# Routing inside the last projection chunk of a hybrid decoder step: one table value per row, expert outputs stored by choice and token

## The reference, cut to what matters

```python
hx = rmsnorm(x, norm_ffn)
g_logits = hx @ w_group + b_group            # 4 groups
grp = argmax(g_logits)
in_grp = (hx @ w_router + b_router)[grp]     # 8 experts of that group
top_v, top_i = top_k(in_grp, 2)
gate = softmax(top_v) * softmax(g_logits)[grp]
# each token goes to 2 of 32 experts; rows of one expert are put together
y_e = (silu(x_e @ w_gate[e]) * (x_e @ w_up[e])) @ w_down[e]
x = rmsnorm(x + gate_0 * y(choice 0) + gate_1 * y(choice 1))
```

## Time and profile before

| what | us |
|---|---|
| median of 3 runs | 1857.71 (1856.18 to 1859.96) |
| the profiled execution | 1851.79 |
| its span in the trace | 1850.0 |
| TensorE busy | 1684.7 (91%) |
| VectorE busy | 876.2 (47%) |
| ScalarE busy | 713.0 (39%) |
| GpSimd busy | 369.2 (20%) |
| HBM read and written | 223.16 MB, 65.51 MB |

### The profile page before, as it was taken

One profiled execution on the slowest core, in us unless ns is written; L12 is line 12 of the kernel. 1 busy time (PEld: TensorE's weight loads), 2 busy tenths in 40 slices (PEclk: granted clock), 3 DMA queues, 4 the chain that ended last, 5 costly groups with the idle time before them and its releaser, 6 DMA issues.

```text
span 1850.0 us, 31840 instructions
## 1 busy us (share of the span) xinstructions
PE 1684.7 (91%) x12271; PEld 1561.5 (84%) x12272; DVE 876.2 (47%) x1663; ACT 713.0 (39%) x1234; POOL 369.2 (20%) x323
## 2 busy tenths in 40 slices
PE   5999999999999999999999979999997299999970
PEld 4998998999989999888887869999997299999960
DVE  5533223123122110555666632345324779999857
ACT  5323223222232222344444432313014178888852
POOL 3001002001002135000000000000012147777744
PEclk7999999999999999999999989999999599999995
DMA  6033303304215325232222232224215199999977
GB/s 189 24 95 101 118 24 117 123 13 160 69 40 184 114 84 170 71 112 68 68 64 76 84 114 93 93 76 157 84 73 230 37 336 380 380 376 378 370 275 271
DMA packets 141568, 272.44 MB, mean 147 GB/s; under 512 B 36068, under 2 KB 106988, under 8 KB 129132
## 3 DMA queue, kind: packets, MB, share of 16 engines
q1 hardware_dynamic: 102688, 202.05, 31.8%
q0 software_dynamic: 19280, 48.93, 7.5%
q10 hardware_dynamic: 19488, 19.87, 3.3%
HBM read 223.16 MB, written 65.51 MB: 156 GB/s over the span
## 4 chain that ended last, share of the span: by engine, by line
PE 80%; DVE 6%; DMA 6%; issue 4%; ACT 2%; DVEq 1%; POOL 1%; SPq 0%; ACTq 0%; POOLq 0%
PE pb L761 19%; PE pb L762 18%; PE pb L763 17%; DMA stage<-in_w_gate_e 4%; PE pw L761 2%; PE pw L763 2%; PE pw L762 2%; PE pq L1099 2%; PE pw L1075 2%; DVE wlo L1703 2%; PE pq L835 2%; PE pw L852 1%; PE pq L761 1%; PE pq L763 1%; PE pq L762 1%
## 5 line engine op out<-in xcount | busy, mean ns | idle before, releaser
L761 PE MATMUL pb<-aTh,wlo 128*128 128x352 f32 x1152 | 384.6, 334 | 17.9 <-DVE aTl L2102 8.1
L761 PE MATMUL pb<-whi,aTl 128*128 128x256 f32 (+1 forms) x1296 | 374.4, 289 | 4.8 <-PE pb L763 2.8
L763 PE MATMUL pb<-aTh,whi 128*128 128x352 f32 x1152 | 371.2, 322 | 0.0
L762 PE MATMUL pb<-aTl,whi 128*128 128x352 f32 x1152 | 370.8, 322 | 0.0
L762 PE MATMUL pb<-wlo,aTh 128*128 128x256 f32 (+1 forms) x1296 | 365.4, 282 | 0.0
L763 PE MATMUL pb<-whi,aTh 128*128 128x256 f32 (+1 forms) x1296 | 363.1, 280 | 0.0
L761 PEld LDWEIGHTS pb<-aTh,wlo 128*128 128x128 f32 x1152 | 217.2, 189 | 48.1 <-issue 34.2
L761 PEld LDWEIGHTS pb<-whi,aTl 128*128 128x128 f32 (+1 forms) x1296 | 232.2, 179 | 17.9 <-issue 8.3
L1703 DVE TENSOR_TENSOR wlo<-stage,whi 128x2048 fp32r<-128x2048 f32 x74 | 169.2, 2287 | 142.0 <-ACT whi L1290 142.0
L763 PEld LDWEIGHTS pb<-whi,aTh 128*128 128x128 f32 (+1 forms) x1296 | 233.4, 180 | 1.0
L762 PEld LDWEIGHTS pb<-wlo,aTh 128*128 128x128 f32 (+1 forms) x1296 | 231.9, 179 | 2.0
(11 more groups left out here) (417 smaller groups left out, 2823.1 us busy)
## 6 DMA issues: line engine op xcount, KB each, us to landing
stg<-in_w_down_e SPq DMA_DIRECT2D x32, 1024.0 KB, 12.3
stage<-in_w_in SPq DMA_DIRECT2D x30, 1024.0 KB, 5.4
stage<-in_w_gate_e SPq DMA_DIRECT2D x16, 1024.0 KB, 12.5
stage<-in_w_up_e SPq DMA_DIRECT2D x16, 1024.0 KB, 12.8
stg<-in_w_gate_e SPq DMA_DIRECT2D x16, 1024.0 KB, 13.0
stg<-in_w_up_e SPq DMA_DIRECT2D x16, 1024.0 KB, 13.7
zg_scratch<-go ACTq DMA_DIRECT2D x48, 176.0 KB, 1.9
sgt<-zg_scratch SPq DMA_DIRECT2D x16, 528.0 KB, 3.5
```

What stands on the lines that cost most here:

```text
L761: pe.matmul(out, ll, rh, start=first, stop=False)
L762: pe.matmul(out, lh, rl, start=False, stop=False)
L763: return pe.matmul(out, lh, rh, start=False, stop=last)
```

## The change

The routing becomes part of the last chunk's loop. Each tile's best group and best two experts (`top_two`) are found three iterations after its projection, its ranks (`rank`) four after. TensorE adds two small products for the ranks (`ranks`) into a spare strip of `ZB` and two that place the rows (`placed`), summed over all tiles. The normalised rows are written in their own iteration instead of one later, the transposes come one iteration earlier, and the router has 36 columns. The table has one value for each row, token + 1 + T * choice, from which both columns of `idx` are made (`tables`): outputs are stored at `choice * T + token`, and `slot` is gone. Group weights, overflow counts and two of the weight splits are put elsewhere in the lists of ScalarE and VectorE. GpSimd clears its buffers before it waits for the table, and its expert loop is written out, with columns of `idx` used in place. In the tail SP reloads the outputs as plain blocks. Only the overflow blocks (experts with over 128 rows) keep the copied lists.

The other edits, as a diff (SP, ScalarE, VectorE's first expert, GpSimd):

```diff
-            sp.wait_ge(init_v, 2)
...
+            sp.wait_ge(m_end, 1)
+            for t in range(NT):
+                if t >= NY:
+                    sp.wait_ge(f_a, t - NY + 1)
+                for k, y in enumerate((y1, y2)):
+                    r = k * T + t * 128
+                    sp.dma_start(y[t % NY][0:rows(t), :], ys_d[r:r + rows(t), :]).then_inc(f_y[t % NY], 16)
...
+                if t == 2:
+                    split_hi(N_MOE, 0, 0, lds(N_MOE))
+                if t == NT - 1:
+                    split_hi(N_MOE + 1, 1, 1, lds(N_MOE + 1))
...
-            for m in range(2):
-                split_hi(N_MOE + m, m, m, lds(N_MOE + m))
-            act.wait_ge(r_v, 1)
-            act.activation(ge[:, :, :], ge[:, :, :], ACT.Exp)
-            act.activation(r1[:, 3, :], r1[:, 2, :], ACT.Exp).then_inc(r_a, 1)
...
-            act.wait_ge(r_v, R_END)
+            act.wait_ge(r_v, R_WGT)
+            act.activation(ge[:, :, :], ge[:, :, :], ACT.Exp)
+            act.activation(r1[:, 3, :], r1[:, 2, :], ACT.Exp).then_inc(r_a, 1)
...
+            x_low(0, 0)
+            weights_of_rows()
             slot_lo(PG(1), 1, 0)
-            slot_lo(PD(0), 0, 2)
-            slot_lo(PU(1), 1, 1)
-            x_low(0, 0)
             gated_half(0)
             x_low(1, 1)
+            slot_lo(PD(0), 0, 2)
             hidden(0)
...
+                if isinstance(e, int):
+                    rows_ = column(0, e)
+                else:
+                    rows_ = ixs[par][:, 0:1]
+                    gp.tensor_copy(ixs[par][:, :], column(0, e)).then_inc(e_ix, 1)
+                    gp.wait_ge(e_ix, e - (NE - 1))
+                    gp.sem_inc(carry[2], 1)
                 gp.indirect_dma_start(out=xg[par][:, :], out_offset=None, in_=h2_d,
-                                      in_offset=bass.IndirectOffsetOnAxis(ap=ixs[par][:, 0:1], axis=0),
+                                      in_offset=bass.IndirectOffsetOnAxis(ap=rows_, axis=0),
...
-            gp.wait_ge(r_v, R_END)
             gp.wait_ge(st_x, 16 * NT)
-            for i in range(2):
-                gp.wait_ge(st_h[i], 16 * ((NT + 1 - i) // 2))
             for x in xg:
                 gp.memset(x[:, :], 0.0)
             gp.drain()
+            for i in range(2):
+                gp.wait_ge(st_h[i], 16 * ((NT + 1 - i) // 2))
+            gp.wait_ge(r_v, R_IDX)
             gather(0, 0)
             gather(1, 1)
             gather(2, 0)
             gather(3, 1)
-            with gp.Fori(0, NE // 2 - 2) as i:
-                gather(2 * i + 4, 0)
-                store_y(2 * i, 0)
-                gather(2 * i + 5, 1)
-                store_y(2 * i + 1, 1)
+            for e in range(NE - 4):
+                gather(e + 4, e % 2)
+                store_y(e, e % 2)
...
-            for t in range(NT):
-                n = rows(t)
-                if t >= NY:
-                    gp.wait_ge(f_a, t - NY + 1)
-                for k, y in enumerate((y1, y2)):
-                    gp.indirect_dma_start(out=y[t % NY][0:n, :], out_offset=None, in_=ys_d,
-                                          in_offset=bass.IndirectOffsetOnAxis(ap=slot[0:n, k, t:t + 1], axis=0),
-                                          bounds_check=2 * T - 1).then_inc(f_y[t % NY], 16)
```

More of the change, by code:

```diff
@@ L40 @@
 NI = 3
-TOP, SC_END = 229344, 214048
+TOP, SC_END, KEEP = 229344, 214048, 139296
 NGRP, EPG, NE, FF = 4, 8, 32, 256
@@ L1265, in _ @@
             with pe.If(any_ > 0):
+                pe.wait_ge(e_yc, E(NE - 1))
+                for a in range(2 * NT):
+                    pe.wait_ge(r_o, NT + a + 1)
+                    pe.matmul(pq[:, 0, 0:NOVER], ORo[a % 2][:, :], OBo[a % 2][:, :], start=(a == 0),
+                              stop=(a == 2 * NT - 1)).then_inc(r_r, 1)
                 with pe.Fori(0, NOVER) as j:
@@ L2146, in _, with bc @@
             ve.memset(onesf[:, :], 1.0)
-            def logits(t):
+            ve.memset(Ac[:, 0, :], 0.0)
+            ve.tensor_scalar(thr[:, :], io[:, 0:8], 128.0, 128.0, ALU.mult, ALU.add)
+            ve.memset(big[:, :], float(2 ** 17))
+            ve.tensor_copy(vt[:, 0, :], C("tokid"))
+            ve.scalar_tensor_tensor(out=vt[:, 1, :], in0=C("valid"), scalar=float(T), in1=C("tokid"),
+                                    op0=ALU.mult, op1=ALU.add)
+            ve.drain()
+            def bc(a, shape, *at):
+                for k in at:
+                    a = a.unsqueeze(k)
+                return a.to_broadcast(shape)
@@ L2224, in _ @@
-            ve.drain()
-            for k in range(2):
-                ve.tensor_tensor(O[:, k, :, :], O[:, k, :, :], bc(C("valid"), [128, NT, NE], 2), ALU.mult)
-            ve.memset(Ac[:, 0, :], 0.0)
-            ve.drain()
-            ve.tensor_tensor(A[:, :, :], O[:, 0, :, :], O[:, 1, :, :], ALU.add)
-            ve.tensor_tensor(Ae[:, :, :], O[:, 0, :, :].rearrange("p t e -> p e t"),
-                             O[:, 1, :, :].rearrange("p t e -> p e t"), ALU.add)
-            ve.drain()
@@ L2323, in _ @@
             ve.tensor_copy(ovt[:, :, :], ovf[:, 0:2, :])
-            for m in range(2):
-                split_lo(N_MOE + m, m, m)
-            ve.wait_ge(r_p, 2)
-            found = pw[:, 0, 0:2 * NBLK].rearrange("p (k b) -> p k b", k=2)
-            ve.tensor_scalar(emp[:, :, :], found, 0.0, big[:, 0:1], ALU.is_equal, ALU.mult)
-            ve.drain()
-            ve.scalar_tensor_tensor(out=idx[:, :, :], in0=found, scalar=-1.0, in1=emp[:, :, :],
-                                    op0=ALU.add, op1=ALU.add)
```

341 lines of the change are left out of this document (152 added, 189 removed).

## The result

The changed kernel takes 1848.37 us (median of five runs, 1847.37 to 1850.22) against 1857.82 of the kernel before: a ratio of 0.9948 (0.9933 to 0.9962). It is 9.5 us faster where 24.3 were forecast; 1848.4 lies above the range of 1826 to 1846. The profiled execution took 1847.37 us with a span of 1845.5.

The account below looks back on a forecast made before the run. The prediction took the serial routing before the first gather as delaying the whole expert stage: 12.9 + 6.7 - 2.0 + 1.0 + 5.7 = 24.3 us off the profiled 1851.8, so 1827.5, or 1833.4 as median; range 1826 to 1846.

Parts of the forecast that it names:

- Part 1: Routing inside the last chunk: 6.6 us a tile, chunk 9.6 us longer, table ready 12.9 us earlier, at 1449.2.
- E: Rival: TensorE and VectorE take turns in the chunk, 12 us an iteration, 32 us lost, 1866; chance 0.03.
- Rival B: In the chunk, GpSimd's power lands after the top-two chain: 8.5 us a tile, 11.4 lost, 1845; chance 0.18.
- Part 2: From the table to the first gathered rows: 6.2 us, a gain of 6.7 us.
- 0.1 + 3.0 + 3.1 us: Table to first gathered rows: time before the indirect DMA, the DMA on GpSimd, then its landing; 6.2 us together.
- the exclusion rule: A VectorE instruction with two SBUF inputs and a GpSimd instruction reading SBUF exclude each other, the later one waiting.
- the upper bound of 11.8 us: Longest time from table to first gathered rows, should the 5.5 us gap ahead of GpSimd's copy come back.
- Part 3: First experts: subtractions moved between VectorE's steps make the weight stream late; 2 us charged, bounds 0 and 4.2.
- Part 4: Tail: 1.0 us gained by a last store without copy, 2.9 before the first combine, 2.8 from first to last.

Follow-up runs that it names:

- early_read: The new kernel with VectorE reading the logits out of PSUM at the start of the iteration, ahead of the projection add: 1838.72 us.
- combined: The new kernel with logits read at iteration start, no clearing of gather buffers, new order after the ninth group, second weight split before the last rank: 1833.88 us.
- warm: combined plus 43 products on TensorE that nobody reads, 10 in the chunk's waits and 33 after the ninth group: 1832.90 us.
- before_no_clear: The kernel before without GpSimd's clearing of the two gather buffers and the drain behind it: 1852.18 us.
- early_sub: The new kernel with three weight subtractions of experts 0 and 1 ahead of the first gathered rows and the overflow counts behind them: 1852.85 us.
- late_subtractions: The kernel before with the three weight subtractions moved behind the first gathered rows, between the steps of experts 0 and 1: 1858.38 us.
- contiguous: The new kernel with each expert's outputs stored to neighbouring rows instead of by choice and token: 1848.58 us.
- one_sub: The new kernel with one weight subtraction (gate chunk of expert 1) ahead of the first gathered rows, overflow counts left in place: 1849.37 us.
- before_again: The kernel before, unchanged, profiled once more: 1853.70 us.

## Why the prediction missed

**Part 1 failed**, in the sentence "The loop hides one behind the other, because the projection group of tile t+1 needs only older adds". The group does, but ahead of it in TensorE's list stand the logits, and they need a read-out of the same VectorE iteration. The one rival that looked for turns between the engines (E) asked only about ranks and groups. Rival B, whose 1845 lies nearest to the result, did not come about: VectorE's scaling follows the last step of the top-two chain without a wait for the power (1405.12 behind 1404.98), so its number is near by chance. The size of the iteration was right once the wait is gone: 6.48 us measured, 6.6 forecast. From the add of tile 0 to the table 73.9 us were forecast and 89.5 came. Of the 15.7 us between them:
- 9.5 are the wait: early_read has 80.0. Of these, 6.4 lie in the chunk (some 1.05 us a tile and one fall of the clock), 3.1 after it.
- 2.4 are the order after the ninth group and the clash of VectorE with the clearing: combined, which has the moved split in the same stretch, has 77.7. Alone, without the earlier read-out, they gave 2.7 and 1.9; part of it was the same wait.
- 2.2 are the clock at tile 4, which every duration of part 1 took as full: warm has 75.4 in its profile.
- 1.6 stay, within what part 1 called bounds.

**The narrower router** saves nothing: 1.95 us for the 16 passes with 36 columns, as with 128 in TensorE's timeline of the kernel before. The forecast had allowed for both.

```profile
1392.39 1.95 PE L1185 MATMUL pq<-wr,h2T 128*128 128x128 f32 x16
```

**Part 2 had the right sum from a wrong reason.** 6.7 us forecast, 6.1 measured. Of its 0.1 + 3.0 + 3.1 us the first term was too small: from the table's last write to the transfer 1.25 us passed (1464.37 to 1465.62). "0.6 us after VectorE has ended three weight subtractions" was a coincidence: without them the gap was the same 5.49 us, and without the clearing it was gone. So the sentence that the exclusion rule agrees with the gap was wrong, and the upper bound of 11.8 us, "should the gap be GpSimd's own and come back", was the nearer thought: it was GpSimd's own, and the change hides it by clearing early. The 2.75 us of the transfer are a wait of the expected kind, behind the weight split.

**Part 3**: the walk through VectorE's list was right (third load 7.8 us after the landing, 7.7 forecast; fourth 15.4 against 15.0). The forecast charged 2.0 us for it. From landing to first combine three profiles of the kernel before and of before_no_clear take 331.8 to 334.6 us, eight of the new kernel and its variants with the same tail (early_sub left out) 332.2 to 335.5; the means are 333.5 and 333.4, although the last store and the reload are shorter in the eight. Up to ScalarE's last write of an expert's output, the three take 319.1 to 321.8 us and the eight 321.9 to 325.5, with means of 320.3 and 323.3. So some 3 us are lost among the experts, and the store and the reload behind that write gain them back. That the order of the subtractions costs these 3 us is not shown: late_subtractions has 323.2 up to that write, but in the slowest of its eleven executions, and its median excludes more than 1.5 us of loss by the order (its interval reaches to 1.0008); contiguous and one_sub found none. What takes the 3 us stays open.

**Part 4 was right in the reload**: 2.4 us gained to the first combine (2.9 forecast) and 3.1 behind it (2.8). The copy that the last store no longer needs was priced too high: from the start of ScalarE's last write to the store 2.1 us passed in the kernel before (1794.05 to 1796.18) and 1.8 pass in the new one (1795.36 to 1797.15), 0.3 gained where 1.0 was forecast. The write in the chain of the kernel before:

```profile
1794.05 1.03 ACT yo L1290
```

The profiled executions differ by 4.4 us and the medians by 9.5, since that of before lay 6.0 below its median and that of the new kernel 1.0. before_again took 1853.7, so part of it is the spread of one execution.

## What to carry to other kernels

When a loop over two engines is made denser, list for every buffer which iteration's read-out frees it, and where in that iteration the read-out stands: one bank less turned a slack of a whole iteration into a wait inside it. Put the instruction that frees a shared buffer first in its engine's iteration. Before an idle gap is put down to the engine that ended beside it, move that engine's work and look whether the gap follows.

## What the hardware showed

- Two clearing instructions on GpSimd that the profile shows with 1.84 us, and the drain behind them, keep its next instruction back 7.3 us (1468.77 to 1476.11, late_subtractions). Without them it starts 0.4 us after the table's last write (before_no_clear).
- In the new kernel's chunk TensorE ran at a granted clock of 1.00 (2.4 GHz) from 1374.85 to 1391.74, busy for 13.31 of 16.89 us, with waits of 1.15 and 1.57 us for normalised rows and of 0.86 for the read-out. Then it ran at 0.51 (1.2 GHz) for 6.86 us without a wait. early_read lacks the third wait, and its clock fell at the same place (0.66 from 1390 to 1400 in both). In warm ten unread products of 128 columns stand in the first two waits, and the clock is 1.00 in the whole chunk.
- A float32 product with 36 moving columns takes TensorE as long as one with 128 (1.95 us for 16 passes at full clock).
